# Third and fourth query-weight slots of each lookup layer loaded ahead into four of the twelve row buffers

## The reference, cut to what matters

```python
def peer_ffn(h, w_q, sub_keys, u_tab, v_tab):          # T = 256, 8 heads, top 16
    q = (xt @ w_q).reshape(T, PEER_HEADS, 2, PEER_HALF)     # w_q: 1024 x 2048
    s = jnp.einsum('thpd,hpnd->thpn', q, sub_keys)          # 128 keys per half
    sv, si = lax.top_k(s, PEER_TOPK)
    cand = sv[:, :, 0, :, None] + sv[:, :, 1, None, :]
    cv, ci = lax.top_k(cand.reshape(T, PEER_HEADS, 256), PEER_TOPK)
    eidx = ...                                    # (T, 128) rows out of 16384
    gates = jax.nn.softmax(cv, axis=-1).reshape(T, 128)
    uc = jnp.take(u_tab, eidx, axis=0)            # a row of 1024 for each token and pick
    vc = jnp.take(v_tab, eidx, axis=0)            # a second row of 1024
    act = jax.nn.gelu(jnp.einsum('cd,ckd->ck', xt, uc))
    return jnp.einsum('ck,ckd->cd', gates * act, vc)
```

## Time and profile before

| | |
|---|---|
| time, median of 3 runs | 2938.89 us (2938.15 to 2939.89) |
| span of the profiled execution | 2936.7 us |
| PE busy | 2611.4 us (89%) |
| DVE busy | 1370.9 us (47%) |
| DMA, mean over the span | 358 GB/s |
| gathered rows (software queue) | 537.56 MB in 512 DMAs |

### The profile page before, as it was taken

The page is one execution under the profiler, slowest core; times in us unless marked ns, Lnnn a source line. Parts: engine busy times, 40 slices in busy tenths (PEclk is TensorE's granted clock), DMA queues, the critical chain, the costliest instruction groups (busy, mean ns, idle before and its releaser), DMA issues.

```text
span 2936.7 us, 28686 instructions
## 1 busy us (share of the span) xinstructions
PE 2611.4 (89%) x9706; PEld 1214.0 (41%) x9706; DVE 1370.9 (47%) x3397; ACT 619.3 (21%) x1242; POOL 490.4 (17%) x526
## 2 busy tenths in 40 slices
PE   8988788887899988778887899899999999999998
PEld 7753333333366653333333366543333232333333
DVE  5747767776525747777776542431111111111111
ACT  3122212232125122222232121211111111111111
POOL 0124333343200124333333200000000000000000
PEclk9999988999999999999999999889999999999999
DMA  5699999999864699999999843448999999899897
GB/s 218 265 421 418 421 421 421 419 418 421 339 242 158 252 408 414 421 422 421 421 422 421 335 146 119 184 175 358 422 422 422 422 422 422 352 422 422 373 404 296
DMA packets 145293, 1049.90 MB, mean 358 GB/s; under 512 B 16272, under 2 KB 16528, under 8 KB 17968
## 3 DMA queue, kind: packets, MB, share of 16 engines
q0 software_dynamic: 74064, 537.56, 44.1%
q1 hardware_dynamic: 70560, 509.12, 42.5%
q10 hardware_dynamic: 576, 2.13, 0.2%
HBM read 1047.69 MB, written 1.05 MB: 357 GB/s over the span
## 4 chain that ended last, share of the span: by engine, by line
PE 53%; DMA 37%; DVE 5%; ACT 2%; issue 1%; DVEq 1%; another core or an unknown queue 1%; SPq 0%; POOLq 0%
DMA uv_more<-in_peer_uv,rows_of 20%; PE psum L570 14%; DMA big<-in_moe 13%; PE psum L980 11%; PE psum L467 7%; PE psum L1006 5%; PE psum L482 5%; DMA big<-in_peer_uv,rows_of 4%; PE psum L892 1%; PE psum L961 1%; DVE uv_more L1613 1%; PE psum L674 1%; PE psum L587 1%; PE psum L974 1%; DVE big L1613 1%
## 5 line engine op out<-in xcount | busy, mean ns | idle before, releaser
L570 PE MATMUL psum<-big,gdiag 128*128 128x512 f32 x1880 | 909.6, 640 | 228.7 <-ACT gdiag L1089 228.5
L1613 DVE CUSTOM_DVE_ANT_0 big<-psum,big 128x1024 f32<-128x1024 f32 x470 | 574.5, 1224 | 278.5 <-DMA big<-in_peer_uv,rows_of 271.9
L570 PEld LDWEIGHTS psum<-big,gdiag 128*128 128x128 f32 x1880 | 374.2, 204 | 755.1 <-issue 438.9
L2031 POOL DMA_INDIRECT big<-in_peer_uv,rows_of x470 | 445.7, 948 | 1143.1 <-PE psum L570 761.4
L980 PE MATMUL psum<-big 128*64 128x512 f32 x2240 | 500.7, 596 | 23.9 <-POOLq L2053 23.2
L1995 DVE TENSOR_SCALAR big<-psum 128x512 f32<-128x512 f32 x35 | 24.2, 692 | 664.2 <-PE psum L980 664.2
L980 PEld LDWEIGHTS psum<-big 128*64 128x64 f32 x2240 | 152.7, 137 | 370.1 <-issue 273.0
L1006 PE MATMUL psum<-ring,big 128*64 128x512 f32 x1120 | 248.0, 594 | 3.7
L467 PE MATMUL psum<-big,ring 128*128 128x256 f32 x1088 | 241.0, 381 | 1.0 <-DVE big L1375 0.9
L467 PEld LDWEIGHTS psum<-big,ring 128*128 128x128 f32 x1088 | 206.1, 191 | 33.9 <-issue 4.8
L1083 ACT ACTIVATE gelu<-dots,rstd 128x4 f32<-128x4 f32 (+1 forms) x134 | 39.8, 297 | 837.5 <-DVE dots L1613 837.5
(11 more groups left out here) (385 smaller groups left out, 1955.4 us busy)
## 6 DMA issues: line engine op xcount, KB each, us to landing
big<-in_moe SPq DMA_DIRECT2D x256, 1024.0 KB, 20.1
ring<-in_moe SPq DMA_DIRECT2D x128, 1024.0 KB, 18.9
big<-in_ada SPq DMA_DIRECT2D x24, 1024.0 KB, 11.9
ring<-in_peer_wq SPq DMA_DIRECT2D x16, 1024.0 KB, 10.5
ring<-in_mix_in SPq DMA_DIRECT2D x14, 1024.0 KB, 7.3
ring<-in_a_in SPq DMA_DIRECT2D x8, 1024.0 KB, 9.3
ring<-in_ple_gate SPq DMA_DIRECT2D x8, 1024.0 KB, 8.8
ring<-in_kv SPq DMA_DIRECT2D x8, 1024.0 KB, 8.6
```

What stands on the lines that cost most here:

```text
L570: mm = pe.matmul(psum[:, OUT_BANK[t] + c, :], gdiag[:, n % DIAGS, :], uv[(PICKS * l + n) % ROWS][:, D + c * 512:D + (c + 1) * 512], start= ...
L1613: j = dve.tensor_tensor_reduce(out=u, in0=x, in1=u, scale=1.0, scalar=0.0, op0=ALU.mult, op1=ALU.add, accum_out=dots[:, n:n + 1])
L2031: pool.indirect_dma_start(uv[g % ROWS], None, table, bass.IndirectOffsetOnAxis(rows_of[:, n:n + 1], 0)).then_inc(uv_loaded[g % ROWS], 16)
```

## The change

The ring no longer takes slots 2 and 3 of `peer_wq`. Both are loaded into row buffers instead: slot 2 into the pair `KEPT[l][0]` (buffers 2 and 3 in layer 0, 1 and 2 in layer 1), slot 3 into `KEPT[l][1]` (1 and 4; 4 and 5). Their loads wait for `mod_turned`. PE reads the two slots' weights from there. The gather starts with the other eight buffers; a table (`row_plan`) says which buffer a pick takes, which earlier pick it must wait for, and for two buffers joining at pick 24 and two at pick 40 that the features of slot 2 or 3 are done. The ring's places are numbered without the two slots (`ring_plan`), so `ple_gate` slots 0 and 1 follow slots 0 and 1 of `peer_wq`.

```diff
+ASIDE = (2, 3)
+EARLY = ((0, 9, 10, 11, 5, 6, 7, 8), (0, 3, 10, 11, 6, 7, 8, 9))
+KEPT = (((2, 3), (1, 4)), ((1, 2), (4, 5)))
+JOIN = (24, 40)
...
+def ring_plan(first, slots):
+    aside = {first[f"peer_q{l}"] + s for l in range(2) for s in ASIDE}
+    place, by_place = {}, {}
+    for n in range(slots):
+        if n not in aside:
+            at, nth = len(place) % RING, len(place) // RING
+            place[n] = (at, nth, by_place.get((at, nth - 1)))
+            by_place[at, nth] = n
+    return place
+
+def row_plan():
+    plan, count = [], [0] * ROWS
+    for l in range(2):
+        free, last, joins = list(EARLY[l]), {}, {}
+        for n in range(PICKS):
+            for which, at in enumerate(JOIN):
+                if n == at:
+                    free = list(KEPT[l][which]) + free
+                    joins = {r: ASIDE[which] for r in KEPT[l][which]} | joins
+            r = free.pop(0)
+            free.append(r)
+            count[r] += 1
+            plan.append((r, count[r], last.get(r), joins.pop(r, None)))
+            last[r] = n
+    return plan
...
             def load(n, src, words=SLOT):
-                b = n - RING
+                b = PLACE[n][2]
                 for f in range(2):
-                    if b >= 0 and f == 0:
+                    if b is not None and f == 0:
                         sp.wait_ge(tile_done, ENDS[b])
                     half(n, f, src, words)
...
             def peer(l):
-                plain(f"peer_q{l}", d["peer_wq"][l])
+                for s in range(2):
+                    load(FIRST[f"peer_q{l}"] + s, d["peer_wq"][l, s])
+                for which, s in enumerate(ASIDE):
+                    sp.wait_ge(mod_turned, 8 * l + which + 1)
+                    for f in range(2):
+                        sp.dma_start(uv[KEPT[l][which][f]], d["peer_wq"][l, s, :, f * ROW:(f + 1) * ROW]).then_inc(
+                            wq_loaded[which], 16)
                 plain(f"ple_gate{l}", d["ple_gate"][l])
...
-                w = slot_in(n, extra).rearrange("p (k f) -> p k f", k=KC)
+                if aside is None:
+                    w = slot_in(n, extra).rearrange("p (k f) -> p k f", k=KC)
+                    ws = [w[:, k, :] for k in range(KC)]
+                else:
+                    l, which = aside
+                    pe.wait_ge(wq_loaded[which], 32 * (l + 1))
+                    ws = [uv[KEPT[l][which][k // 4]].rearrange("p (k f) -> p k f", k=4)[:, k % 4, :] for k in range(KC)]
...
@@ gpsimd
                     g = PICKS * l + n
-                    if n == 7 and l == 0:
+                    r, _, before, kept = ROW_PLAN[g]
+                    if n == 6 and l == 0:
                         pool.wait_ge(mod_turned, 4)
+                    if kept is not None:
+                        pool.wait_ge(tile_done, ENDS[FIRST[f"peer_q{l}"] + kept] - 2)
                     if n % TOPK == 0:
                         pool.wait_ge(rows_ready, g // TOPK + 1)
-                    if n >= ROWS:
-                        pool.wait_ge(v_done, g - ROWS + 1)
-                    pool.indirect_dma_start(uv[g % ROWS], None, table,
+                    if before is not None:
+                        pool.wait_ge(v_done, PICKS * l + before + 1)
+                    pool.indirect_dma_start(uv[r], None, table,
```

More of the change, by code:

```diff
@@ L117, in build @@
     FIRST, ENDS, TILE_ENGINE, TILE_NTH = stream_plan()
+    PLACE = ring_plan(FIRST, len(ENDS))
+    ROW_PLAN = row_plan()
     def tile0(stage):
@@ L304, in build @@
         keys_loaded = sem("keys_loaded")
+        wq_loaded = [sem(f"wq_loaded{s}") for s in ASIDE]
         x_back, rows_ready, gexp_in, gexp_out = sem("x_back"), sem("rows_ready"), sem("gexp_in"), sem("gexp_out")
@@ L366, in half @@
             def half(n, f, src, words=SLOT):
-                at = f * words // 2
-                sp.dma_start(ring[:, n % RING, at:at + words // 2], src[:, at:at + words // 2]).then_inc(
-                    loaded[2 * (n % RING) + f], 16)
+                at, place = f * words // 2, PLACE[n][0]
+                sp.dma_start(ring[:, place, at:at + words // 2], src[:, at:at + words // 2]).then_inc(
+                    loaded[2 * place + f], 16)
             def load(n, src, words=SLOT):
-                b = n - RING
+                b = PLACE[n][2]
                 for f in range(2):
-                    if b >= 0 and f == 0:
+                    if b is not None and f == 0:
                         sp.wait_ge(tile_done, ENDS[b])
@@ L447, in slot_in @@
             def slot_in(n, extra=0, halves=(0, 1)):
+                at, nth, _ = PLACE[n]
                 for f in halves:
-                    pe.wait_ge(loaded[2 * (n % RING) + f], extra + 16 * (n // RING + 1))
-                return ring[:, n % RING, :]
+                    pe.wait_ge(loaded[2 * at + f], extra + 16 * (nth + 1))
+                return ring[:, at, :]
             def bank_free(m):
@@ L455, in bank_free, with features @@
                     pe.wait_ge(act_took if TILE_ENGINE[m - 3] == "A" else dve_took, TILE_NTH[m - 3])
-            def features(stage, s, rhs, free=bank_free, extra=0, n=None, between=None):
+            def features(stage, s, rhs, free=bank_free, extra=0, n=None, between=None, aside=None):
                 n = FIRST[stage] + s if n is None else n
-                w = slot_in(n, extra).rearrange("p (k f) -> p k f", k=KC)
+                if aside is None:
[5 more added lines that the diff above has]
+                    ws = [uv[KEPT[l][which][k // 4]].rearrange("p (k f) -> p k f", k=4)[:, k % 4, :] for k in range(KC)]
                 m = ENDS[n - 1] if n else 0
@@ L466, in features @@
                         for k in range(KC):
-                            mm = pe.matmul(psum[:, (m + t) % 3, f * T:(f + 1) * T], w[:, k, c:c + P], rhs[:, k, :],
+                            mm = pe.matmul(psum[:, (m + t) % 3, f * T:(f + 1) * T], ws[k][:, c:c + P], rhs[:, k, :],
                                            start=(k == 0), stop=(k == KC - 1))
@@ L570, in mix_rows @@
                         mm = pe.matmul(psum[:, OUT_BANK[t] + c, :], gdiag[:, n % DIAGS, :],
-                                       uv[(PICKS * l + n) % ROWS][:, D + c * 512:D + (c + 1) * 512],
+                                       uv[ROW_PLAN[PICKS * l + n][0]][:, D + c * 512:D + (c + 1) * 512],
                                        start=(at == 0), stop=(at == PICKS // TT - 1), skip_group_check=True)
@@ L612, in peer @@
                 for s in range(1, 4):
-                    features(f"peer_q{l}", s, xT, between=mix_inside(s) if s in inside else None)
+                    features(f"peer_q{l}", s, xT, between=mix_inside(s) if s in inside else None,
+                             aside=(l, ASIDE.index(s)) if s in ASIDE else None)
                     if s == 1 and l == 0:
@@ L1610, in peer @@
                         g = PICKS * l + n
-                        dve.wait_ge(uv_loaded[g % ROWS], 16 * (g // ROWS + 1))
-                        u = uv[g % ROWS][:, 0:D]
+                        r, nth, _, _ = ROW_PLAN[g]
+                        dve.wait_ge(uv_loaded[r], 16 * nth)
+                        u = uv[r][:, 0:D]
                         j = dve.tensor_tensor_reduce(out=u, in0=x, in1=u, scale=1.0, scalar=0.0, op0=ALU.mult,
@@ L2024, in _ @@
                     g = PICKS * l + n
-                    if n == 7 and l == 0:
+                    r, _, before, kept = ROW_PLAN[g]
+                    if n == 6 and l == 0:
                         pool.wait_ge(mod_turned, 4)
+                    if kept is not None:
+                        pool.wait_ge(tile_done, ENDS[FIRST[f"peer_q{l}"] + kept] - 2)
                     if n % TOPK == 0:
                         pool.wait_ge(rows_ready, g // TOPK + 1)
-                    if n >= ROWS:
-                        pool.wait_ge(v_done, g - ROWS + 1)
-                    pool.indirect_dma_start(uv[g % ROWS], None, table,
+                    if before is not None:
+                        pool.wait_ge(v_done, PICKS * l + before + 1)
+                    pool.indirect_dma_start(uv[r], None, table,
                                             bass.IndirectOffsetOnAxis(rows_of[:, n:n + 1], 0)).then_inc(
-                                                uv_loaded[g % ROWS], 16)
+                                                uv_loaded[r], 16)
             pool.wait_ge(hs_ready, 16)
```

## The result

The changed kernel takes 2946.81 us (median of 11 runs, 2942.66 to 2954.03), the kernel before 2939.58 us beside it (11 runs, 2934.24 to 2944.20). The ratio is 1.0024, interval 1.0014 to 1.0034: slower by 7.1 us, 4.1 to 10.0. The forecast was 2947.8 us, range 2940 to 2953.

The account below looks back on a forecast made before the run. The full DMA engines were taken as the bound, with PE's order pacing each lookup's first 90 us. Layer 0's 3.9 us and layer 1's 5.0 us added 8.9 us to 2938.89: 2947.8 us, range 2940 to 2953.

Parts of the forecast that it names:

- The bytes: Slots 2 and 3, 9.96 us of DMA time per layer, move to the idle stretch before the gather, over 15 us cover.
- PE's order is the clock: First 90 us of a lookup: PE's fixed mixing places pace the gather; picks 4 to 7 stay at 164.75 us.
- Two picks fewer at the restart: Restart at 220.7 us in layer 0: 26 picks are out where 28 were; pick 26 is issued then.
- The idle time: Layer 0 before the restart: DMA engines idle about 14 us, in three gaps beginning near 182, 195 and 217 us.
- a gap near 1049 us in layer 1: Sign of being right: DMA share also falls near 1049 us, early in layer 1's gather.
- The sizes: After the restart: pick 32 in layer 0 lands 3.9 us later, layer 1 runs 5.0 us later; sum 8.9 us.
- The restart's latency: Landing time of a pick issued to empty engines at the restart: taken as 5.4 us from the nearest row.
- Rival B: Layer 1: PE's 4.5 us stall goes, restart comes 4.5 us earlier; +4.4 us, 2943.3 us, no measurable difference; chance 0.11.
- Rival A: Full stretch of the gathers: freed bytes are gained, 9.96 us per layer, 19.9 us faster, 2919.0 us; chance 0.07.

Follow-up runs that it names:

- the execution with the stall: First profile of the kernel before, nothing changed: PE stood 4.5 us idle after layer 1's slot 1 features; layer 1's gather took 654.1 us.
- the second profile: The kernel before profiled once more, unchanged: PE waited 0.69 us at that place; layer 1's gather took 650.9 us.
- the first pair of profiles: First profiles of the kernel before and the changed kernel: layer 1's gather 654.1 and 655.7 us.
- The second pair: Both kernels profiled once more, unchanged: layer 1's gather 650.9 us in the kernel before, 655.9 us in the changed one.

## Why the prediction was right

*The bytes.* The two slots went into the empty stretch, landed 5.0 to 8.9 us after they were issued, long before PE wanted slot 2 at 146.28 us, and nothing waited for them. Right.

*PE's order is the clock.* Each mixing stands within 0.2 us of before. This was the step on which everything else rests, and it held to the wait of 1.05 us.

*Two picks fewer at the restart.* Right, and pick 26 was issued 0.2 us after pick 28's old time.

*The idle time.* About 14 us in three gaps were forecast; the idle time rose by 14.1 us in layer 0 (15.7 against 1.6), in gaps that begin near 180, 195 and 218 us (forecast 182, 195 and 217). One sign failed: a gap near 1049 us in layer 1, 41 us after its pick 0, did not open; the share there is 0.99 to 1.02. The forecast had read layer 1's places from the execution with the stall, where pick 12 was issued 27.2 us after pick 0; in the second profile it is 22.3 us. The sum did not use it.

*The sizes.* Layer 0: forecast +3.9 us, pick 32 landed 4.5 us later, and the gather was 3.2 to 3.8 us longer. Layer 1: forecast +5.0 us; 655.7 and 655.9 us against 650.9, 4.8 to 5.0 us. The sum by gathers is 8.0 to 8.8 us for a forecast 8.9. That the whole kernel came within 1 us of its forecast is in part luck: the interval of the difference is 3 us to either side, and outside the gathers the profiles of one kernel differ by up to 5 us.

*The restart's latency.* Pick 26 went out to engines that nothing else used, which no row before showed. Its own rows, of line 2088, against the earlier trace rows:

```profile
L2088 POOL DMA_INDIRECT big<-in_peer_uv,rows_of x1: 936/936/936, 220.9 to 220.9; - x1
...
DMA to landing us min/median/max: 5.5/5.5/5.5
```

So 5.5 us where I had taken 5.4. The rule of the Trainium skill (DMA: Bandwidth & Descriptors, Anatomy of one DMA — SWDGE (gpsimd) path), 4.4 us by estimate, is 1.1 us short for this gather of 8 KiB rows.

*What I read wrongly.* Rival B took the 4.5 us stall of layer 1 for something that the change might remove. It was in one execution of the kernel before and in no other profile. In the first pair of profiles it does look like B: layer 1's gather is only 1.6 us longer. The second pair is 4.9 us apart in that gather. The medians of the runs differ by 7.1 us, which fits the second pair; what the runs without a profile did there is not shown. Rival A names the gain that is really there; it needed another order on PE and ACT together with the moved weights.

## What to carry to other kernels

Taking work off the resource that bounds a stretch pays only if the stretch's other clock lets the rest of the work move up: here that was PE's hand-written order, and bytes left out alone gave 7 us, the order alone nothing, and bytes moved ahead with the order, buffers that join in time and ACT's diagonals first gave 18. Before a buffer is lent to something else, count the pieces in flight when the next long pause begins: two picks fewer were 3.5 to 5 us a layer, and giving the buffers back as soon as they were free took that back with one line. A stall that stands in one profile should be looked for in a second one before it becomes a term or a rival.

## What was unexpected about the hardware

A gather of 1 MiB in 128 rows took 5.5 to 5.7 us from issue to landing with the engines empty, and 2.49 us a piece in a row. In one execution the feature matmuls of one slot were followed by 4.5 us of waiting with the granted clock at 1.00 up to its end and down to 0.50 right behind it, and in the nine other profiles by 0.7 us; its cause stays open. Between executions of the kernel before the time moved by 10 us (2934 to 2944), while the gathers, bound by the DMA engines, differed by 0.4 us at most between two profiles of one kernel, apart from that stall.
